# Sixteen and twelve starting places for the split weights inside their ring slots

## The reference

```python
def conv_ffn(h, w_up, conv_w, conv_b, w_down):
    u = h @ w_up
    a, g = u[..., :D_FF], u[..., D_FF:]
    a = dwconv_centred(a, conv_w, conv_b)
    return (jax.nn.gelu(a) * g) @ w_down
...
    for l in range(DEPTH):
        h = h + hybrid_mixer(rms_norm(h, mix_norm_g[l]), w_in[l], ...)
        h = h + memory_cross_attention(rms_norm(h, xattn_norm_g[l]), rms_norm(mem, mem_norm_g[l]), ...)
        h = h + conv_ffn(rms_norm(h, ffn_norm_g[l]), w_up[l], ffn_conv_w[l], ffn_conv_b[l], w_down[l])
    return rms_norm(h, final_norm_g)
```

## Time and profile before

| | |
|---|---|
| median of the runs | 878.94 us (878.68 to 879.21) |
| span of the profiled execution | 878.1 us |
| outside the span, against the median | 0.8 us |
| TensorE matmuls, share of the span | 98% |
| weight loads / VectorE / ScalarE | 91% / 68% / 57% |
| mean granted TensorE clock | 0.998 |
| DMA | 146.78 MB, mean 167 GB/s |

### The profile page before, as it was taken

One profiled execution on the slowest core, in us unless ns is written; L12 is line 12 of the kernel. 1 busy time (PEld: TensorE's weight loads), 2 busy tenths in 40 slices (PEclk: granted clock), 3 DMA queues, 4 the chain that ended last, 5 costly groups with the idle time before them and its releaser, 6 DMA issues.

```text
span 878.1 us, 14940 instructions
## 1 busy us (share of the span) xinstructions
PE 863.8 (98%) x6334; PEld 799.8 (91%) x6334; DVE 596.2 (68%) x820; ACT 496.8 (57%) x689; POOL 16.8 (2%) x35
## 2 busy tenths in 40 slices
PE   8999999999999999999999999999999899999997
PEld 7999998889889999999999999988898899999996
DVE  6788588757657666656567875887656666656655
ACT  7864673648647445445577546745755645445444
POOL 5100000000000000000000000000000000000000
PEclk9999999999999999999999999999999999999999
DMA  8825453364255555555448254325425365555541
GB/s 312 234 74 168 167 168 121 101 235 145 97 192 193 192 192 192 193 192 192 145 146 256 68 174 161 139 101 192 146 96 191 129 207 192 192 194 191 192 169 48
DMA packets 114665, 146.78 MB, mean 167 GB/s; under 512 B 10600, under 2 KB 94760, under 8 KB 114600
## 3 DMA queue, kind: packets, MB, share of 16 engines
q1 hardware_dynamic: 114456, 145.57, 50.3%
q10 hardware_dynamic: 144, 0.26, 0.1%
HBM read 144.77 MB, written 1.05 MB: 166 GB/s over the span
## 4 chain that ended last, share of the span: by engine, by line
PE 92%; ACT 3%; DVE 3%; issue 1%; DMA 0%; ACTq 0%; DVEq 0%
PE bank L665 25%; PE bank L666 25%; PE bank L667 25%; PE bank L706 4%; PE bank L743 2%; PE bank L832 2%; DVE wlo L1455 2%; PE bank L1017 2%; PE bank L762 1%; ACT whi L1096 1%; ACT yhi L1119 1%; PE bank L872 1%; PE bank L849 1%; DVE ylo L1710 1%; PE bank L882 1%
## 5 line engine op out<-in xcount | busy, mean ns | idle before, releaser
L1455 DVE TENSOR_TENSOR wlo<-raw,whi 128x2048 fp32r<-128x2048 f32 (+3 forms) x144 | 306.3, 2135 | 104.6 <-ACT whi L1096 103.8
L1096 ACT ACTIVATE whi<-raw 128x2048 fp32r<-128x2048 f32 (+3 forms) x144 | 257.7, 1794 | 53.3 <-PE bank L667 48.3
L665 PE MATMUL bank<-yhi,whi 128*128 128x256 f32 x704 | 195.4, 277 | 0.5 <-DVE ylo L1471 0.5
L666 PE MATMUL bank<-ylo,whi 128*128 128x256 f32 x704 | 194.8, 277 | 0.0
L667 PE MATMUL bank<-yhi,wlo 128*128 128x256 f32 x704 | 194.8, 277 | 0.0
L665 PEld LDWEIGHTS bank<-yhi,whi 128*128 128x128 f32 x704 | 132.4, 188 | 1.7 <-issue 0.7
L666 PEld LDWEIGHTS bank<-ylo,whi 128*128 128x128 f32 x704 | 132.2, 188 | 0.8
L667 PEld LDWEIGHTS bank<-yhi,wlo 128*128 128x128 f32 x704 | 132.2, 188 | 0.0
L665 PE MATMUL bank<-xhi,whi 128*128 128x256 f32 x320 | 91.6, 286 | 1.7 <-DVE wlo L1455 1.3
L665 PE MATMUL bank<-whi,xhi 128*128 128x512 f32 (+2 forms) x256 | 90.1, 352 | 0.0
L667 PE MATMUL bank<-xhi,wlo 128*128 128x256 f32 x320 | 89.0, 278 | 0.0
(11 more groups left out here) (268 smaller groups left out, 1378.2 us busy)
## 6 DMA issues: line engine op xcount, KB each, us to landing
raw<-in_w_up SPq DMA_DIRECT2D x44, 1024.0 KB, 5.0
raw<-in_w_down SPq DMA_DIRECT2D x22, 1024.0 KB, 4.8
raw<-in_w_in SPq DMA_DIRECT2D x10, 1024.0 KB, 6.7
raw<-in_w_xk SPq DMA_DIRECT2D x8, 1024.0 KB, 5.2
raw<-in_w_xv SPq DMA_DIRECT2D x8, 1024.0 KB, 5.0
raw<-in_w_out SPq DMA_DIRECT2D x8, 1024.0 KB, 4.9
raw<-in_w_xq SPq DMA_DIRECT2D x8, 1024.0 KB, 5.4
raw<-in_w_xo SPq DMA_DIRECT2D x8, 1024.0 KB, 5.0
```

Of the source, the lines that this page charges most:

```text
L665: mm(o, s_hi, m_hi, start=first, stop=False, skip_group_check=True)
L666: mm(o, s_hi, m_lo, start=False, stop=False, skip_group_check=True)
L1096: A(weight(whi, gu), raw[:, gu % RING, 0:SIZE[gu]], ACT.Copy).then_inc(hi_done, 1)
L1455: tt(weight(wlo, gu), raw[:, gu % RING, 0:SIZE[gu]], weight(whi, gu), ALU.subtract).then_inc(lo_done, 1)
```

## The change

Each unit gets a starting place of its own, from two lists that are gone through in turn: the n-th held unit takes `HELD_AT[n % 16]`, the n-th moving unit `MOVING_AT[n % 12]`. The numbers are float32 elements, so they are multiples of 16 bytes. `raw`, the activations, the number of instructions, their order and their waits stay as they are.

```diff
 RING = 3
 UW = 2048
+HELD_AT = (16, 0, 8, 24, 32, 40, 48, 64, 80, 96, 112, 128, 4, 12, 20, 56)
+MOVING_AT = (0, 8, 16, 24, 32, 48, 64, 80, 96, 112, 128, 4)
+PLACE, _met = [], [0, 0]
+for *_, _nk, _ in UNITS:
+    _held = int(_nk == KT)
+    PLACE.append((MOVING_AT, HELD_AT)[_held][_met[_held] % (len(MOVING_AT), len(HELD_AT))[_held]])
+    _met[_held] += 1
...
         def weight(w, gu):
 
-            o = HALF if UNITS[gu][3] == KT else 0
+            o = PLACE[gu]
             return w[:, gu % RING, o:o + SIZE[gu]]
```

## The result

The kernel after takes 897.11 us (896.91 to 897.30, two runs) beside 878.94 us: the ratio is 1.0203, with a 95% interval of 1.0186 to 1.022. That is 18.2 us slower, outside the range that was forecast (872 to 893), and about where the rival "a worse rhythm at most places" was priced (893 to 898). The interval reaches over the 2% line, so it is not shown on which side of 2% the loss lies. `split_mm` now stands at L672 to L674, `fm_alternating` at L713, the split at L1462.

What follows compares the result with a forecast made beforehand. TensorE's cadence, how far apart two matmuls start, was taken as the bound. Span 878.1 + 3.8 (held units) + 1.6 (boundaries) = 883.5 us; the median stands 0.8 above, forecast 884, range 872 to 893.

Steps and rivals of the forecast that it cites:

- a worse rhythm at most places: Rival: TensorE's fast held cadence needs 64 bytes between operands, 12 of 16 places lose it; 893 to 898 us, chance 0.15.
- The steps on what the change leaves alone: SyncE's queue, POOL and `raw` see nothing; ScalarE's and VectorE's work, with the split into `wlo`, costs 0 more.
- Held units, level: Held matmuls on TensorE: each unit's start draws fast or slow level, half and half; +3.8 us, bounds -4.8 to +18.4.
- Moving units, level: Cadence of the 1104 moving 512-column matmuls on TensorE: taken as 0, bounds -12 to +14.4 us.
- Unit boundaries: Where the place changes between units, a handful of slower TensorE matmuls may come again: +1.6 us, bounds 0 and +4.9.
- The place doesn't matter: Rival: stalls and switches set TensorE's rhythm, addresses only shift it; 878 to 880 us, chance 0.32.
- The faster rival: A changed place breaks TensorE's lasting slow level, -4.8 us, 874; with faster moving units 870; chance 0.15.

Runs made afterwards that it cites:

- e1: Kernel after, but only held units go through their sixteen places, all moving units at 0: 892.85 us, ratio 1.0145 to the kernel before.
- e6: Kernel after, but all held units at place 0 and all moving units at 0: 897.96 us, ratio 1.0208 to the kernel before.
- e2: Kernel after, but only moving units go through their twelve places, all held units at 16: 884.94 us, ratio 1.0054 to the kernel before.
- e3: Kernel after, but held units alternate between 16 and 80, moving units go through 0, 64, 128: 878.93 us, ratio 0.9992 to the kernel before.
- e11: Kernel after, but moving units go through all 64 places of a 256-byte period, held units at 16: 885.26 us, one run.
- e4: Kernel after, but 192 empty bytes ahead of `h` shift all activations, held units at 0, moving at 48: 880.25 us, ratio 1.0006 to the kernel before.
- e8: Kernel before (held 16, moving 0), but with five held units at place 56: 881.02 us, ratio 1.0012.
- e10: Kernel after, but all held units at place 22 and all moving units at 0: 879.87 us, ratio 0.9998 to the kernel before.

## Why the prediction was wrong

The steps on what the change leaves alone held: no instruction, wait or DMA was added, the split stayed at 2.29 us at every place, those off the 64-byte grid included, and the chain stayed on TensorE. (Two readings there were off without a part in the miss: TensorE waited for the split ten times, 5.4 us, not seven times, 4.5 us; and by the starts 21% of the steady held matmuls were in the slow level, not the 28% that the rounded means gave.)

**The step that failed is "Held units, level".** It took every unit's start for a new draw between 113.3 and 118 ns, half and half, +3.8 us. Measured: +13.1 us of cadence in the trace, and +12.8 us in e1 by the ratio. The reasoning behind it was that equal addresses ran at two levels, so the address doesn't choose. That is half true. The distance between the operands fixes which levels a unit can have (113.3 or 117.8 at 64 bytes, 120 alone at 0, and so on). Among them something else chooses, which differs from run to run. The trace before holds one distance per kind of unit, so it could show the second half only, and I priced the first at nothing. The number that was right stood beside it as a bound: all at 120 ns, +18.4 us, against +18.3 us in e6. That the bound comes so near the change's +18.2 us too is in part luck: the change has not all held matmuls at 120 ns, and the moving units make up for it.

**"Moving units, level"** was taken at 0, between +14.4 and -12 us. It was +3.8 us in the trace after and +3.5 us of e2's +4.7. The right value lay between 0 and the upper bound: at the change's nine places that are no multiple of 256 bytes the 512-column matmuls take 230.4 to 233.5 ns. The lower one, from L1017 in the earlier trace rows, was of another format (float32, not fp32r) and nothing came near it.

**"Unit boundaries"**, +1.6 us, has no counterpart: e3 has as many jumps, by 256 and 512 bytes, and costs nothing; and in e11, where each moving unit jumps to another distance, the held matmuls behind them have 4.0 us above 113.3 ns, where those of the kernel before have 4.1.

**The rivals.** "A worse rhythm at most places" is what happened, with the price and the time nearly as written. Its rule for the places was part right: 12 of 16 held places were to lose 6.7 ns and the odd multiples of 64 bytes none, but 48 and 112 lost 3.5 as well. 14 of 16 lost between 2.3 (56) and 5.7 ns (64, 128) against the 114.3 that the steady matmuls at 16 averaged before. For 898 a third of the moving units was to lose 13 ns, and 9 of 12 places lost 3 to 6. It had a chance of 0.15. Its evidence was in the rows, namely that the moving units at distance 0 pay twice the overhead of the held ones at 64 bytes; I discounted it since 118 ns occurs at 64 bytes as well. "The place doesn't matter" is refuted by e6. With it go the two sentences of the Trainium skill that it leaned on. e6 differs from the kernel before in nothing but 64 bytes, stays on multiples of 16 bytes and costs 2.08%: the 16-byte line of "SBUF — State Buffer" (section on the DMA port swizzle) doesn't describe it. And against "TensorE: Matmul & The Clock Gate", Part 2, step 1, by which loading the next weights takes no SBUF read bandwidth from the running matmul, e6 is 2.0% slower than e4, each beside the kernel before (1.0208 and 1.0006), though both have their held units at place 0: what differs for them is how far the operand that is loaded lies from the one that streams. That the two reads get in each other's way is the likely reading; the runs show the dependence and not the way. The faster rival found no support: other places reach 113.3 ns, but none goes below it, and e8 and e10 gained nothing.

What stays open is the mechanism: why 64 bytes, and 13, 19, 22 and 51 numbers, are good and their neighbours aren't, and what decides between two levels at one place.

## What to carry to other kernels

Here, where TensorE is busy with fp32r matmuls of 256 and 512 columns 98% of the time, each with a weight load of its own, the distance modulo 256 bytes between what is loaded and what streams was worth 2% of the time, and choosing it costs nothing. Another kernel of this kind can be surveyed as here: a few places in a single run, with several units at each, since one unit may show either of two levels. A trace in which an operand has only ever stood at one place says nothing of what another place costs; a level that comes in two kinds at one address doesn't show that the address is innocent. Where the trace has only one setting of what is changed, the far bounds of a term deserve a large share of the chance.

## What the runs showed of the hardware beside this

The profiled run of the kernel after has a stretch early on in which the granted clock is near half of full, the 1.2 GHz level, and which the kernel before's run lacks. Stretches of both (length, busy time and count by engine, granted clock, DMA share, GB/s), first of after, where TensorE's columns alone were asked for, then of before:

```profile
24.00:28.70 4.70, 4.70 (x29) 1.00 0.17 34
28.70:32.40 3.70, 3.70 (x19) 0.54 0.88 249
```
```profile
24.00:29.40 5.40, 5.40 (x34) 4.23 (x33) 3.92 (x8) 2.24 (x6) 2.14 (x4) 1.00 0.62 183
29.40:32.40 3.00, 3.00 (x27) 2.97 (x27) 1.40 (x2) 3.00 (x5) 0.00 (x0) 1.00 0.91 160
```

Ahead of the fall TensorE had done 29 matmuls in 4.7 us, few beside the 27 in 3.0 us later on; the kernel before did about as few, 34 in 5.4 us, and its clock stayed at full. By their starts the held matmuls stood 213 ns apart at half clock, so the 17 of them cost 17 x (213 - 120) = 1.6 us of after's span, by no doing of the change. The same stretch is there in the profiled runs of e1, e3 and e8 and in no other; e2, e6 and e10 had done 29, 30 and 28 matmuls in the same 4.7 us, and their clock stayed at full. So the count of matmuls ahead of it doesn't tell by itself. The stretch may be part of the scatter of the kernel before over its 51 runs beside the experiments (877.5 to 881.9 us): the 23 with a mean granted clock of 0.998 or 0.999 average 878.9 us, the other 28 average 880.5, and the 1.6 us between them is what the stretch costs. The two go together; that one causes the other isn't shown, since no trace of these 51 runs was kept.
